# The norms' inverse root moved into the transposing product, their gain or shift into the split, x finished later

## The reference

```python
def first_block(x, ...):
    for l in range(DEPTH):                                   # DEPTH = 2
        y = token_mixer(x, ...)
        x = layer_norm(ALPHA * x + y, ln_g[l, 0], ln_b[l, 0])
        y = swiglu(x, ...) if l % 2 == 0 else moe_ffn(x, router_w, router_b, w13, w2)
        x = layer_norm(ALPHA * x + y, ln_g[l, 1], ln_b[l, 1])
    return x

def second_block(x, ...):
    for l in range(DEPTH):
        h = rms_norm(x, norm_mix_g[l]);  x = x + mixer(h) @ w_out[l]
        h = rms_norm(x, norm_ffn_g[l]);  x = x + conv_ffn(h)
    return rms_norm(x, final_g)

def layer_norm(x, g, b):   # y = (x - mean) * rsqrt(var + 1e-5) * g + b, over the 1024 channels
def rms_norm(x, g):        # y = x * rsqrt(mean(x * x) + 1e-6) * g
```

## Time and profile before

| | |
|---|---|
| median of 3 runs | 2420.73 us (2419.69 to 2421.21) |
| profiled execution, whole | 2413.6 us |
| its span, in which the rows count | 2411.8 us |
| mean granted clock of TensorE | 0.966 |
| TensorE busy with matmuls | 2286.6 us (95%) |
| VectorE, ScalarE, GpSimd busy | 1750.6, 1322.5, 182.3 us |
| read from memory | 554 MB, 230 GB/s over the span |

### The profile page before, as it was taken

The page is one execution under the profiler, slowest core; times in us unless marked ns, Lnnn a source line. Parts: engine busy times, 40 slices in busy tenths (PEclk is TensorE's granted clock), DMA queues, the critical chain, the costliest instruction groups (busy, mean ns, idle before and its releaser), DMA issues.

```text
span 2411.8 us, 41151 instructions
## 1 busy us (share of the span) xinstructions
PE 2286.6 (95%) x16277; PEld 2139.7 (89%) x16277; DVE 1750.6 (73%) x1881; ACT 1322.5 (55%) x1253; POOL 182.3 (8%) x178
## 2 busy tenths in 40 slices
PE   7998999999699999999999999999699999898998
PEld 7998998999689999999999999999588999887997
DVE  4565545457478888888888888888677777667777
ACT  4643443554266767676776777677345444425443
POOL 1000000100000000000000000000390000750000
PEclk9998999999699999999999999999899999879999
DMA  9344655534289999999999999999433555323541
GB/s 303 106 148 133 207 177 170 172 114 159 78 301 340 350 334 349 333 351 353 334 349 332 350 334 351 335 349 341 141 105 115 175 196 175 128 88 122 198 174 56
DMA packets 423432, 556.44 MB, mean 231 GB/s; under 512 B 9746, under 2 KB 377092, under 8 KB 423344
## 3 DMA queue, kind: packets, MB, share of 16 engines
q1 hardware_dynamic: 419232, 544.85, 66.5%
q0 software_dynamic: 4112, 10.38, 1.4%
HBM read 554.13 MB, written 1.06 MB: 230 GB/s over the span
## 4 chain that ended last, share of the span: by engine, by line
issue 46%; PE 42%; DVE 6%; ACT 3%; DVEq 2%; DMA 1%; ACTq 0%; SPq 0%; POOL 0%; POOLq 0%
PE ps L618 12%; PE ps L619 12%; PE ps L620 12%; DVE w_lo L1697 2%; ACT w_hi L1312 2%; PE ps L1188 1%; PE ps L660 1%; DVEq L2164 1%; DVE cvT L2163 0%; PE ps L809 0%; DMA raw<-in_w_in 0%; DVE xn L1733 0%; PE ps L1186 0%; DVE x L1791 0%; PE ps L801 0%
## 5 line engine op out<-in xcount | busy, mean ns | idle before, releaser
L1697 DVE TENSOR_TENSOR w_lo<-raw,w_hi 128x2048 fp32r<-128x2048 f32 x519 | 1180.0, 2284 | 348.6 <-ACT w_hi L1312 347.1
L1312 ACT ACTIVATE w_hi<-raw 128x2048 fp32r<-128x2048 f32 x519 | 987.3, 1909 | 246.6 <-PE ps L620 236.3
L618 PE MATMUL ps<-w_hi,xg_hi 128*128 128x256 f32 x1792 | 515.0, 287 | 9.9 <-DVE xg_lo L2073 7.1
L618 PE MATMUL ps<-xT_hi,w_hi 128*128 128x256 f32 (+1 forms) x1712 | 494.2, 289 | 11.2 <-DVE xT_lo L1707 6.7
L620 PE MATMUL ps<-w_hi,xg_lo 128*128 128x256 f32 x1792 | 503.8, 281 | 0.0
L619 PE MATMUL ps<-w_lo,xg_hi 128*128 128x256 f32 x1792 | 503.3, 281 | 0.0
L619 PE MATMUL ps<-xT_lo,w_hi 128*128 128x256 f32 (+1 forms) x1712 | 489.4, 286 | 0.0
L620 PE MATMUL ps<-xT_hi,w_lo 128*128 128x256 f32 (+1 forms) x1712 | 489.0, 286 | 0.0
L618 PEld LDWEIGHTS ps<-w_hi,xg_hi 128*128 128x128 f32 x1792 | 338.4, 189 | 17.4 <-issue 11.1
L618 PEld LDWEIGHTS ps<-xT_hi,w_hi 128*128 128x128 f32 (+1 forms) x1712 | 332.7, 194 | 16.3 <-issue 8.8
L619 PEld LDWEIGHTS ps<-w_lo,xg_hi 128*128 128x128 f32 x1792 | 338.9, 189 | 4.0
(11 more groups left out here) (442 smaller groups left out, 2795.6 us busy)
## 6 DMA issues: line engine op xcount, KB each, us to landing
raw<-in_exp_w SPq DMA_DIRECT2D x336, 1024.0 KB, 5.6
raw<-in_ffn_w_up SPq DMA_DIRECT2D x44, 1024.0 KB, 5.0
raw<-in_w_in SPq DMA_DIRECT2D x42, 1024.0 KB, 6.9
raw<-in_ffn_w SPq DMA_DIRECT2D x33, 1024.0 KB, 4.9
raw<-in_ffn_w_down SPq DMA_DIRECT2D x22, 1024.0 KB, 5.3
raw<-in_w_gate SPq DMA_DIRECT2D x16, 1024.0 KB, 5.3
raw<-in_w_out SPq DMA_DIRECT2D x8, 1024.0 KB, 4.8
raw<-in_w_o SPq DMA_DIRECT2D x6, 1024.0 KB, 5.6
```

The lines of the kernel that those rows point to most:

```text
L618: pe.matmul(out, lhs[0], rhs[0], start=first, stop=False)
L1312: act.activation(w_hi[:, u.const % SPL, 0:width], raw[:, u.const % RAW, 0:width], ACT.Copy)\
L1697: dve.tensor_tensor(w_lo[:, u.const % SPL, 0:width], raw[:, u.const % RAW, 0:width], w_hi[:, u.const % SPL, 0:width].bitcast(F32), ALU.sub ...
```

## The change

Five things change.

1. The root goes into the transposing. VectorE writes `dg` = identity * root for each tile of tokens (128x128), and `transpose_x` multiplies x by dg instead of by the identity, so that what arrives in PSUM is transposed and scaled; only the very first transposing stays plain. At places 1 to 3 the shift b is added when `x_parts` reads PSUM, by channel, which is then a column (`beta`); at places 4 to 7 the gain g is multiplied there (`gain`). These columns are loaded by seven DMAs of 128x8 single values, issued in layer 0 after `norm_gb`. `x_parts` works by 256 columns instead of 512.
2. x itself is finished later: at places 1 to 3 `normed_x` (times root, plus b, four quarters) runs after `x_parts` (at place 2 after `split(u + 1)` as well) and raises the new `ln_done`.
3. The squares of the RMS norms go from VectorE to ScalarE (`square_roots`), each started by its quarter's `x2_ready`, and the root is taken there for one tile at a time.
4. GpSimd's loads for mixer1 of layer 1 and for the router wait for `ln_done` instead of `xn_ready`. The loads of the RMS norms' gains, spread over the partitions, are gone.
5. Where a stage starts with a norm (places 2, 5, 6 and 7), ScalarE splits the second unit of the stage after `x_parts` instead of before the norm.

```diff
 def transpose_x(ready, first, plain=False):                       # TensorE
...
-                            m = pe.transpose(o[:, c, t, :], src[:, t, (2 * b + c) * P:(2 * b + c + 1) * P], ident)
+                            piece = x[:, t, (2 * b + c) * P:(2 * b + c + 1) * P]
+                            if plain:
+                                m = pe.transpose(o[:, c, t, :], piece, ident)
+                            else:
+                                m = pe.matmul(o[:, c, t, :], piece, dg[:, t, :], start=True, stop=True)
...
 # GpSimd
-                pool.wait_ge(S_.xn_ready, L * 4 + 2)
+                if L:
+                    pool.wait_ge(S_.ln_done, 2)
...
-                pool.wait_ge(S_.xn_ready, L * 4 + 4)
+                if L == 0:
+                    column = lambda dst, v: pool.dma_start(dst, v.rearrange("(c p) -> p c", p=P), ...).then_inc(S_.beta_loaded, 16)
+                    for n, v in enumerate((A["ln_b"][0, 0], A["ln_b"][0, 1], A["ln_b"][1, 0])):
+                        column(beta(n), v)
+                    for l in range(2):
+                        column(gain(2 * l), A["norm_mix_g_2"][l])
+                        column(gain(2 * l + 1), A["norm_ffn_g_2"][l])
+                pool.wait_ge(S_.ln_done, 2 * L + 1)
...
+            def square_roots(count, quarters=QUARTERS):            # ScalarE
+                act.activation(stat[:, 8:9], ones[:, 0:1], ACT.Sqrt)
+                for q, (t, h) in enumerate(quarters):
+                    at = 122 + 2 * t + h
+                    act.wait_ge(S_.x2_ready, count + q + 1)
+                    act.activation(xn[...], x[:, t, h * HALF:(h + 1) * HALF], ACT.Square, accum_out=stat[:, at:at + 1])
+                    act.drain()
+                    if h == 0:
+                        act.activation(stat[:, 126 + t:127 + t], stat[:, at:at + 1], ACT.Copy, scale=1.0 / D, bias=RMS_EPS)
+                    else:
+                        act.activation(stat[:, 120 + t:121 + t], stat[:, at:at + 1], ACT.Sqrt, scale=1.0 / D,
+                                       bias=stat[:, 126 + t:127 + t]).then_inc(S_.roots_done, 1)
...
 # VectorE
             def layer_norm(count, norms, at, n):
+                centre(norms, at, n)
+                centred(0)
+                root_ready(count)
+                diagonals().then_inc(S_.xn_ready, 1)
+                centred(1).then_inc(S_.xn_ready, 1)
+            def normed_x():
+                finished(0)
+                finished(1).then_inc(S_.ln_done, 1)
+            def rms_norm(n):
+                for t in range(TT):
+                    dve.wait_ge(S_.roots_done, TT * n + t + 1)
+                    dve.reciprocal(col(120 + t), col(120 + t))
+                    dve.drain()
+                    m = dve.tensor_scalar(dg[:, t, :], ident, col(120 + t), None, ALU.mult)
+                m.then_inc(S_.xn_ready, 2)
```

More of the change, by code:

```diff
@@ L1381, in out @@
                     act.activation(dst, src, ACT.Copy).then_inc(S_.proj1_out, 1)
-                x_parts(L * 8, 4)
+                x_parts(L * 8, 4, beta(1) if L else None)
+                if L:
+                    split(u + 1)
                 for n in range(2):
@@ L1565, in mixer2 @@
             def mixer2(L, u):
-                square_root(S_.sqrt2_in, S_.sqrt2_out, L * 5 + 1, stat[:, 120:122])
-                x_parts(L * 8 + 16, 4)
+                square_roots(8 * L, QUARTERS if L else NORM_ORDER)
+                x_parts(L * 8 + 16, 4, scale=gain(2 * L))
+                if L:
+                    split(u + 1)
                 def ahead(n):
@@ L1668, in _ @@
             act.activation(bvec[:], ps[0:HA, 0, 0:BUCKET_W], ACT.Copy).then_inc(S_.bvec_ready, 1)
-            for n in range(AHEAD):
-                split(Count(n))
+            split(Count(0))
+            split(Count(1))
             for L in range(2):
@@ L1701, in used, with x_parts @@
                 dve.wait_ge(S_.unit_used, u.value(plus=SPL + 1))
[L1703 removed]
+            def x_parts(count, first, shift=None, scale=None):
                 for b in range(4):
                     dve.wait_ge(S_.xT_hi_ready, count + b + 1)
[L1706 to L1708 removed]
+                    if shift is None and scale is None:
+                        m = dve.tensor_tensor(xT_lo[:, 2 * b:2 * b + 2, :], bank(first + b, 2, S),
+                                              xT_hi[:, 2 * b:2 * b + 2, :].bitcast(F32), ALU.subtract)
+                    else:
+                        for c in range(2):
+                            k = 2 * b + c
+                            hi, i = xT_hi[:, k, :].bitcast(F32), bank(first + b, 2, S)[:, c, :]
+                            if shift is not None:
+                                m = dve.scalar_tensor_tensor(xT_lo[:, k, :], i, shift[:, k:k + 1], hi, ALU.add, ALU.subtract)
+                            else:
+                                m = dve.scalar_tensor_tensor(xT_lo[:, k, :], i, scale[:, k:k + 1], hi, ALU.mult, ALU.subtract)
+                    m.then_inc(S_.xT_lo_ready, 1)
             def y_parts(first, dst, hi, ready, count, done):
@@ new lines, in finished, with diagonals, layer_norm @@
+            def finished(h):
+                for t in range(TT):
+                    m = dve.scalar_tensor_tensor(quarter(t, h), quarter(t, h), col(120 + t), norm_gb[:, 1, h * HALF:(h + 1) * HALF],
+                                                 ALU.mult, ALU.add)
+                return m
+            def diagonals():
+                for t in range(TT):
+                    m = dve.tensor_scalar(dg[:, t, :], ident, col(120 + t), None, ALU.mult)
+                return m
+            def layer_norm(count, norms, at, n):
+                centre(norms, at, n)
[3 more added lines that the diff above has]
+                centred(1).then_inc(S_.xn_ready, 1)
@@ L1859, in mixer1 @@
                 dve.memset(xmT[:, :, 0:CONV_K - 1], 0.0)
-                x_parts(L * 12, 4)
+                x_parts(L * 12, 4, beta(1) if L else None)
                 split(u + 1)
+                if L:
+                    normed_x()
                 split(u + 2)
```

173 lines of the change are left out of this document (86 added, 87 removed).

## The result

The changed kernel takes 2402.7 us (median of 7 runs, 2400.78 to 2404.03), against 2419.65 for the kernel before in the same comparison (7 runs, 2411.11 to 2421.21): a ratio of 0.9942, 95% interval 0.9929 to 0.9955. Forecast were 2427.7 us, slower, with a range of 2420 to 2433.5. The change is 14 us faster by the ratio, 10.9 us between the two profiled executions (2413.6 and 2402.7).

What follows compares the result with a forecast made beforehand. TensorE, busy 2286.6 of 2411.8 us, was taken as the bound, so only its waits or added work count. Losses 9.5 less gains 2.6 gave +6.9 us on the 2420.73 median: 2427.7 us, range 2420 to 2433.5.

Steps and rivals of the forecast that it cites:

- The losses: Places 2 and 3: loads and router held up by what was moved behind normed_x, together 9.5 us.
- Place 3: Router's loads wait until normed_x ends, so the router starts 6.8 us later; bounds 5.5 and 8.
- Place 2: Ten loads wait for ln_done, so b_if lands after the value products' start: loss 2.7 us, bounds 1.2 and 5.2.
- rival 4: Experts: the router's delay is given back if the stream of weights bounds them; 2420.9 us; chance 0.08.
- rival 1: Places 5 to 7: clock stays up behind waits of 2.8 us, saving 6 us more; 2421.7 us, not slower; chance 0.20.
- places 5 to 7: Waits of 2.8 us, clock at 0.50 behind them, product 5.48 us: gains 0 and 1.5, then loss 0.4.
- The product's two records for a square: Transposing with dg: 32 records for 16 squares, 5.48 us after a wait against 3.65, +1.8 us at each of seven places.
- rival 3: Transposing with dg: four passes, 14.6 instead of 5.5 us at seven places, +64 us, about 2490; chance 0.02.
- the loads of columns: Layer 0, behind b_if: seven loads of 1024 pieces of 4 bytes, taken as 0, bounds 0 and 5.4 us.
- rival 2: Column loads cost 3 to 5 us at the start, or place 2 its 5.2: 2432 us; chance 0.12.
- the split moved behind xT_hi: Places 2, 5, 6, 7: second unit's split ends at S + 5.3, before T(1) at S + 5.8; cost 0, bound 1 us each.

Runs made afterwards that it cites:

- p1_second_block_only: Changed kernel with the first block's layer norms as before and only the second block's RMS norms changed: 2395.08 us, ratio 0.9907 to the kernel before.
- e1_early_loads: Changed kernel with GpSimd's mixer1 and router loads waiting for xn_ready, only gain and shift loads for ln_done: 2392.56 us, ratio 0.9907 to the kernel before.
- e4: Changed kernel with the seven column loads made contiguous, 128 pieces of 32 bytes each instead of 1024 of 4: 2400.98 us.
- e5: Changed kernel with the plain transposing of x by the identity at places 4 to 7, leaving the root out: 2398.23 us.
- e6: Changed kernel with three filler products (2.05 us) on VectorE between reciprocal and diagonal at place 4 alone: 2408.89 us.
- b1: Changed kernel with loads no longer behind ln_done, and normed_x at place 3 behind the split of the router's weights: 2385.73 us, ratio 0.9886 to the kernel before.
- e7: Changed kernel with x times root written by VectorE and a plain transposing at places 4 to 7: 2412.43 us, ratio 0.9991 to the kernel before.
- e3: Changed kernel with one filler product on VectorE between second reciprocal and second diagonal at places 5 to 7: 2413.66 us, ratio 0.9984 to the kernel before.
- c2: Kernel before with three filler products (2.05 us) on VectorE ahead of xn at place 4 alone: 2410.97 us, ratio 0.9977 to the kernel before.
- e2: Changed kernel with three filler products on VectorE between second reciprocal and second diagonal at places 5 to 7: 2416.72 us, ratio 1.0004 to the kernel before.
- c1: Kernel before run again, no edit, for a second profile and its spread: 2413.36 us, ratio 1.000.

## Why the prediction was wrong

*The losses were right in kind and place, and somewhat small.* Place 3: GpSimd's first load was issued at 636.83, and TensorE began the router at 643.61, 6.1 us later than before if the 2.7 us already lost are taken off; forecast 6.8. The rest of its 8.2 us came behind it, in a longer stretch at half clock.

```profile
636.83 0.53 POOL L568 DMA_DIRECT2D norm_gb<-in_ln_g  x1 [196.28 <-DVE x L1798]
637.86 0.90 POOL L571 DMA_DIRECT2D rw_raw<-in_router_w  x1
```

Place 2: the value products waited for b_if. They began 1.0 us later than before, 2.5 with the 1.5 already gained; forecast 2.7. They then ran at half clock, 3.65 us for 1.89:

```profile
446.35 3.65 PE L788 MATMUL ps<-xmT,wqk 128*128 128x256 f32 x8 [4.07 <-DMA b_if<-in_b_if]
```

These 1.8 us are what was missing to the 4.2. (By the recorded rows the forecast itself should have said 2.5, which is 447.9 less 445.37, and the slack of the last load is 7.5 us and not 2.5; the sum would be 0.2 lower.) p1_second_block_only and e1_early_loads show both losses to be real: 11.6 us by the one, 11.7 given back by the other. Within the experts 0.2 us were made up before the last unit, and 1.4 at that one, where before the clock had been down 3.4 us longer; rival 4 is out.

*The step that failed* is the one in rival 1: "So the fall comes late, but it comes; in the product it would only come later and cost the same." I had taken it from a single wait of 2.88 us and made half clock a certainty behind waits of 2.8. The fourteen profiles of this case give, for places 5 to 7, the clock in the transposing behind the wait:

| wait before the transposing, us | kernels | clock stayed up |
|---|---|---|
| 2.55 to 2.59 | changed (2 profiles), e1, e4, e5, p1, e6, b1 | 22 of 24 |
| 3.14 to 3.18 | e7 | 2 of 3 |
| 3.32 to 3.71 | e3 | 1 of 3 |
| 4.6 to 6.1 | before (2 profiles), c2, e2 | 0 of 12 |

So the wait was rightly forecast (2.8; it is 2.55), and its first effect too; the forecast charged each product 5.48 us behind it where 3.81 was due. Places 5 to 7 came out 8.9 us better, more than rival 1's 6. Of the 2.9 us between, 2.6 are the second fall some 25 us behind places 5 and 7, which neither the forecast nor rival 1 had. That the shorter wait keeps the clock up is shown by e2_wait_longer, which has all else of the change, has the clock down at all three places and is no faster than the kernel before. So places 5 to 7 are worth 10.0 us instead of 1.1 because the change takes three waits below the length behind which the clock mostly falls.

*The second error is no step of the sum but a term that it lacked.* The kernel before stands for 24 to 27 us at half clock in one or both mixers of the second block, at 7.7 to 8.6 us each; the changed kernel did so in none of its two profiles. The profiled execution had one, worth 9 of the 10.9 us: without it the two executions would be some 2 us apart, since places 2 and 3 lose 12.4 us and places 5 to 7 gain 10.0. Of the seven runs of the kernel before that the result was compared with, five lie in the upper group (2417.9 to 2421.2); against the two lower ones the gain is 9.6 us and not 14. c1, c2, e4 and e7 show that this is not tied to the change: it moves between layers of one kernel, comes less often when work is added, and comes back in variants of the changed kernel. Why it is rare in the changed kernel is open. The range had no room for it, though the page before has it in its row of clocks (tenths, 40 slices of 60 us); the 36th slice is that mixer. That row before, then after:

```profile
PEclk9998999999699999999999999999899999879999
```

```profile
PEclk9999999999789999999999999999889999989999
```

The 7 of the 36th slice says that 24 to 36 us at half clock lay in it.

The product's two records for a square were right: at full clock it takes 3.81 us against 1.94 for the plain transposing, 1.96 times as long and not four times (rival 3); how many passes a record holds no run here shows. Also right were the loads of columns at nothing in the end (rival 2) and the split moved behind xT_hi: T(1) starts without a wait for w_lo at places 2, 5, 6 and 7. In the mixer of layer 0, 1.3 us were lost by a step that I did not have: VectorE's scan of `cumT` takes 2.64 us and took 1.42, with GpSimd at work in both, and the next w_lo was 1.4 us later. Before, then after:

```profile
1749.77 1.42 DVE L2214 TENSOR_TENSOR_SCAN cumT<-cst,laT 128x256 f32<-128x256 f32 x2
```

```profile
1758.49 2.64 DVE L2276 TENSOR_TENSOR_SCAN cumT<-cst,laT 128x256 f32<-128x256 f32 x2
```

This is a lead for the long stretches too. In layer 0 four profiles have the short scan and a wait for `st` of 3.5 us behind it (before, c1, c2, e4), and three of them have the long stretch there; ten have the long scan and a wait of 4.3 to 5.3 us, and one of them (e7) has it. That the one causes the other isn't shown.

## What to carry to other kernels

A wait of the matrix engine has two prices: its length, and the clock behind it. Look in the trace for waits just above the length behind which the clock still stays; shortening such waits by 2 to 3 us gave 1.8 to 3.9 each, and lengthening them by 2.3 to 2.7 cost 3.9 to 5.5. When a step is put off to shorten one path, list everything that hangs on its semaphore: here loads that did not need the finished x waited for it, and letting them go was worth 10 us, with one more reordering 17. And where the runs of the kernel before fall in two groups, profile it twice before a single execution's rows are made the base of a sum.

## What the runs showed of the hardware that was not expected

- Behind the wait for `st` in the mixers of the second block (1.4 to 5.3 us) the clock stayed at half for 3.4, 6.8 or 10.2 us in some executions and for 23.9 or 27.3 in others of the same kernel, with TensorE busy in nearly all of it.
- Behind one and the same wait of 3.32 us the clock stayed once and fell once; behind 2.55 to 2.59 it fell in 2 of 24.
- A fall of the clock was mostly not the only one: behind 10 of 12 falls at places 5 and 7 a second one of 3.4 us came some 25 us later, worth 1.3 us.
- 2.05 us of added VectorE work on the path made the kernel before 5.6 us faster by the ratio.
- A float32 product of 128x128 squares with a float32 diagonal makes two records a square and takes 3.81 us for 16 squares at full clock and 5.15 to 6.32 us where the clock fell, against 1.94 for the plain transposing at full clock.
